# Two transformer-style blocks on one core: norm roots taken from the bank, sums of ones put into TensorE's waits, and six smaller moves

## The reference, cut to what matters

```python
y = xf * lax.rsqrt(jnp.mean(xf * xf, axis=-1, keepdims=True) + EPS)      # each norm
hx = modulate(rmsnorm(x, norm_g[l]), shift[:, None], scale[:, None])
# odd layer
u, g = jnp.split(h @ p["w_in"], [W_POOL], axis=-1)
d = multiscale_pool(u.reshape(bn * rows, GRID_W, W_POOL)).reshape(bn, n, W_POOL)
y = jnp.einsum("bngi,gij->bngj", d, p["w_grp"]) * p["scale"]
x = x + gate * ((y * jax.nn.silu(g)) @ p["w_out"])
# second block
mix_x, _, _ = token_mixers(h @ w_in[l], ...)    # forward and backward chunked recurrence
x = x + mod[:, 2, None] * mix_x
h2 = modulate_2(rmsnorm_2(x, g_ffn[l]), mod[:, 3, None], mod[:, 4, None])
x = x + mod[:, 5, None] * swiglu(h2, w_up[l], w_down[l])
return rmsnorm_2(x, g_final)
```

## Time and profile before

| | us |
|---|---|
| median of the runs | 942.37 |
| profiled execution, its own time | 943.91 |
| its span, first to last instruction | 942.1 |
| TensorE busy (matrix products) | 891.3 (95%) |
| VectorE busy | 704.2 (75%) |
| ScalarE busy | 498.2 (53%) |
| GpSimd busy | 142.5 (15%) |
| mean granted TensorE clock | 0.974 of full |

### The profile page before, as it was taken

One profiled execution on the slowest core, in us unless ns is written; L12 is line 12 of the kernel. 1 busy time (PEld: TensorE's weight loads), 2 busy tenths in 40 slices (PEclk: granted clock), 3 DMA queues, 4 the chain that ended last, 5 costly groups with the idle time before them and its releaser, 6 DMA issues.

```text
span 942.1 us, 17236 instructions
## 1 busy us (share of the span) xinstructions
PE 891.3 (95%) x7064; PEld 833.2 (88%) x7064; DVE 704.2 (75%) x1017; ACT 498.2 (53%) x710; POOL 142.5 (15%) x254
## 2 busy tenths in 40 slices
PE   7999999998997699999999999979999799999995
PEld 5788777688997699989999999979999799999995
DVE  5687578999877599978579985776995876566553
ACT  5374888896544445325553574554534454444441
POOL 0004674710011001400212100300001000000000
PEclk8899999999998799999999999989999799999998
DMA  9935977986575668866628744625566466666661
GB/s 366 359 135 143 311 262 227 294 303 222 174 258 180 218 201 263 297 216 193 185 85 312 269 151 129 213 90 179 161 187 174 142 217 184 187 182 180 201 201 45
DMA packets 56013, 195.43 MB, mean 207 GB/s; under 512 B 7936, under 2 KB 9088, under 8 KB 54528
## 3 DMA queue, kind: packets, MB, share of 16 engines
q1 hardware_dynamic: 40320, 147.73, 49.2%
q0 software_dynamic: 15616, 46.61, 14.4%
HBM read 188.60 MB, written 1.05 MB: 201 GB/s over the span
## 4 chain that ended last, share of the span: by engine, by line
PE 67%; DVE 15%; ACT 7%; DMA 5%; issue 3%; POOL 2%; SPq 0%; DVEq 0%; ACTq 0%; POOLq 0%
PE ps L571 19%; PE ps L572 19%; PE ps L573 19%; DVE w_lo L1336 5%; PE ps L724 3%; ACT w_hi L944 2%; DMA m<-in_mod_w 2%; DMA raw<-in_stream 2%; POOL shifts L459 2%; PE px L644 1%; DMA modw<-in_mod_w 1%; PE ps L655 1%; DVE modw L1370 1%; DVE win L1350 1%; DVE dump L1706 1%
## 5 line engine op out<-in xcount | busy, mean ns | idle before, releaser
L1336 DVE TENSOR_TENSOR w_lo<-raw,w_hi 128x1024 fp32r<-128x1024 f32 x232 | 280.9, 1227 | 120.1 <-ACT w_hi L944 119.6
L944 ACT ACTIVATE w_hi<-raw 128x1024 fp32r<-128x1024 f32 x232 | 243.6, 1056 | 123.5 <-DMA raw<-in_stream 123.3
L571 PE MATMUL ps<-h_hi,w_hi 128*128 128x256 f32 (+1 forms) x928 | 278.5, 300 | 24.7 <-DVE w_lo L1336 13.5
L572 PE MATMUL ps<-h_lo,w_hi 128*128 128x256 f32 (+1 forms) x928 | 273.3, 295 | 0.0
L573 PE MATMUL ps<-h_hi,w_lo 128*128 128x256 f32 (+1 forms) x928 | 273.0, 294 | 0.0
L571 PEld LDWEIGHTS ps<-h_hi,w_hi 128*128 128x128 f32 x928 | 181.4, 195 | 37.2 <-DVE w_lo L1336 18.0
L572 PEld LDWEIGHTS ps<-h_lo,w_hi 128*128 128x128 f32 x928 | 181.5, 196 | 3.7 <-issue 1.2
L573 PEld LDWEIGHTS ps<-h_hi,w_lo 128*128 128x128 f32 x928 | 181.3, 195 | 2.8
L571 PE MATMUL ps<-h2o_hi,w_hi 128*128 128x256 f32 x352 | 102.1, 290 | 0.0
L573 PE MATMUL ps<-h2o_hi,w_lo 128*128 128x256 f32 x352 | 100.0, 284 | 0.0
L572 PE MATMUL ps<-h2o_lo,w_hi 128*128 128x256 f32 x352 | 99.9, 284 | 0.0
(11 more groups left out here) (332 smaller groups left out, 1736.7 us busy)
## 6 DMA issues: line engine op xcount, KB each, us to landing
raw<-in_stream SPq DMA_DIRECT2D x252, 512.0 KB, 3.9
modw<-in_mod_w POOLq DMA_DIRECT2D x80, 512.0 KB, 5.8
m<-in_mod_w SPq DMA_DIRECT2D x8, 1024.0 KB, 19.2
shifts<-upad POOLq DMA_DIRECT2D x128, 35.5 KB, 4.0
c_row<-in_c_rows SPq DMA_DIRECT2D x3, 512.0 KB, 6.1
ctxT<-in_ctxT SPq DMA_DIRECT2D x1, 1024.0 KB, 5.1
x<-in_xT SPq DMA_DIRECT2D x1, 1024.0 KB, 7.1
ctx2T<-in_ctx2T SPq DMA_DIRECT2D x1, 1024.0 KB, 6.6
```

What stands on the lines that cost most here:

```text
L571: pe.matmul(o, wh, hi, start=start, stop=False)
L572: pe.matmul(o, wh, lo, start=False, stop=False)
L944: act.activation(w_hi[split[0] % HI_RING][:], raw[n % RING][:], ACT.Copy).then_inc(w_hi_ready, 1)
L1336: v.tensor_tensor(w_lo[n % RING][:], raw[n % RING][:], w_hi[split[0] % HI_RING][:].bitcast(F32), ALU.subtract).then_inc(w_lo_ready, 1)
```

## The change

1. The norm's root for three norms (after `yb`, after `wo`, after `d2`) and for the context's norm is taken by ScalarE straight from the bank, with the scale and the small constant in the same instruction (`root_of_mean`); VectorE's scaling pass and one hand-over go. The root's table is loaded ahead of the squares (`root_table`).
2. `keep_busy(n)` puts n products of ones with ones (128 x 128) on TensorE: 18 of them in the start, and 4 before and 14 behind the sums of the norms after `yb` and `wo`.
3. ScalarE takes the first four `ou` tiles and the first two `ua` tiles out of their banks before the splits of later weights; two splits are run ahead of that.
4. `add_to_x` for the last tile of a layer (except `ob`) no longer runs the split of four tiles later first.
5. `keys_out(1, 0)` stands ahead of the copies of `o 2`, `o 3` and `ga2 0`.
6. VectorE splits `ou 6` and `ou 7` right behind the first `pooled`; in the feed-forward part it splits two more tiles before `mod_tiles(18, 0)`, and the four dot products of `mod_tiles(19, 0)` stand in the loop, one each at t = 2 to 5.
7. At the end ScalarE multiplies `x` by the last gain while TensorE still works (`xg`), VectorE multiplies by the reciprocal in three pieces, and three DMAs store them instead of eight.

```diff
@@ SyncE
-            for k in range(KT):
-                sp.wait_ge(stored, k + 1)
-                sp.dma_start(out[:, k, :], x[:, k, :]).then_inc(out_done, 16)
+            for n, (first, end) in enumerate(((0, 2), (2, 5), (5, 8))):
+                sp.wait_ge(stored, n + 1)
+                sp.dma_start(out[:, first:end, :], xg[:, first:end, :]).then_inc(out_done, 16)
@@ TensorE
+            def keep_busy(n, bank=px[1]):
+                for _ in range(n):
+                    pe.matmul(bank[:, 0:P], ones, ones, start=True, stop=True)
...
-            first_rows(0)
-            first_columns(0)
-            first_rows(1)
-            first_columns(1)
+            for k in range(2):
+                first_rows(k)
+                keep_busy(2, ps[3])
+                first_columns(k)
             for k in range(KT):
+                if k < 3:
+                    keep_busy((4, 8, 2)[k], ps[3])
                 if k + 2 < KT:
                     first_rows(k + 2)
...
+            keep_busy(4)
             two_chunks(px[0], sq1, 1, KT)
+            keep_busy(14)
...
+            keep_busy(4)
             two_chunks(px[0], sq4, 7, 5 * KT)
+            keep_busy(14)
@@ ScalarE
+            def root_table():
+                S.do(act.activation(warm, warm, ACT.Sqrt))
+            def root_of_mean(stat, t, bank):
+                act.wait_ge(stat_done, stat)
+                act.activation(t, bank[:, 0:T], ACT.Sqrt, scale=1.0 / D, bias=eps_col).then_inc(sd_ready, 1)
...
+            root_table()
             for t in range(KT):
                 done("yb", t)
                 squares("yb", t, sq1)
-            highs("ou", 3)
-            sqrt_of(4, vr1[:])
+            root_of_mean(5, vr1[:], px[0])
             shifted(0, h1_hi, t1, shift1)
             act.wait_ge(pads_ready, 1)
+            highs("ou", 5)
             for t in range(2 * KT):
-                done("ou", t)
+                if t < 4:
+                    act.wait_ge(tile_done, TILE[("ou", t)] + 1)
+                else:
+                    done("ou", t)
...
-            sqrt_of(8, lnv[:, 3, :])
+            sqrt_of(4, lnv[:, 3, :])
+            keys_out(1, 0)
+            highs("ga2", 2)
             out_of("o", 2, og2, ACT.Silu)
             out_of("o", 3, og2, ACT.Silu)
             out_of("ga2", 0, ga2, ACT.Sigmoid)
-            keys_out(1, 0)
...
             for t in range(KT):
                 done("d2", t)
                 squares("d0", t, sq5)
-            sqrt_of(11, v4[:, 0, :])
+                act.activation(xg[:, t, :], x[:, t, :], ACT.Identity, scale=col("g_final_2", t)).then_inc(xg_ready, 1)
+            root_of_mean(10, v4[:, 0, :], px[0])
@@ VectorE
             def add_to_x(name, t, gate):
-                done(name, t)
+                if t < KT - 1 or name == "ob":
+                    ahead(name, t)
+                v.wait_ge(tile_done, TILE[(name, t)] + 1)
...
-            def rstd(stat, bank, width, eps, t, dst, var_n):
-                v.wait_ge(stat_done, stat)
-                v.tensor_scalar(t, bank, 1.0 / width, eps, ALU.mult, ALU.add).then_inc(var_ready, 1)
-                v.wait_ge(sd_ready, var_n)
+            def rstd(n, t, dst):
+                v.wait_ge(sd_ready, n)
                 S.do(v.reciprocal(dst, t))
...
+            lows("ub", 2)
             mod_tiles(18, 0)
-            ahead("ua", 0)
-            mod_tiles(19, 0)
...
+                if 2 <= t < 6:
+                    mod_tiles(19, 0, t - 2, 1)
...
-            for k in range(KT):
-                v.scalar_tensor_tensor(out=x[:, k, :], in0=x[:, k, :], scalar=col("g_final_2", k), in1=v4[:, 1, :],
-                                       op0=ALU.mult, op1=ALU.mult).then_inc(stored, 1)
+            v.wait_ge(xg_ready, KT)
+            for first, end in ((0, 2), (2, 5), (5, 8)):
+                by_token = v4[:, 1, :].rearrange("p (n t) -> p n t", n=1).to_broadcast([P, end - first, T])
+                v.tensor_tensor(xg[:, first:end, :], xg[:, first:end, :], by_token, ALU.mult).then_inc(stored, 1)
```

More of the change, by code:

```diff
@@ L295, in build @@
         sq5 = at("sq5", W, [KT, T])
+        xg = at("xg", W + 8, [KT, T])
         ps = [ctx.enter_context(nc.psum_tensor(f"ps{j}", [P, 2 * T], F32)) for j in range(BANKS)]
@@ L362, in build @@
         out_done = sem("out_done")
+        xg_ready = sem("xg_ready")
         modA = columns(2 * KT).rearrange("p (k w) -> p k w", w=2)
@@ L595, in side_by_side @@
                             mm.then_inc(tile_done, 1)
+            def keep_busy(n, bank=px[1]):
+                for _ in range(n):
+                    pe.matmul(bank[:, 0:P], ones, ones, start=True, stop=True)
             pe.wait_ge(cc_clear, 2)
-            for n in range(12):
-                pe.matmul(px[n % 2][:, 0:P], ones, ones, start=True, stop=True)
+            keep_busy(12, ps[3])
             stats(px[2], lambda k: sq0[:, k, :], 0, sq0_ready)
@@ L858, in _ @@
             thirds("ga2", 0, *own2)
-            pe.wait_ge(var_ready, 6)
+            pe.wait_ge(var_ready, 4)
             pe.wait_ge(hg_dve, 10)
@@ L888, in _ @@
             pe.wait_ge(in_sgu, 48)
-            pe.wait_ge(var_ready, 7)
+            pe.wait_ge(var_ready, 5)
             for g in range(HEADS):
@@ L1123, in sqrt_of @@
                 S.n += 1
-                act.wait_ge(var_ready, n - 2)
+                act.wait_ge(var_ready, n)
                 S.sync()
                 act.activation(t, t, ACT.Sqrt).then_inc(sd_ready, 1)
-            sqrt_of(3, lnt[:, 3, :])
+            sqrt_of(1, lnt[:, 3, :])
             highs("gb", 5)
@@ L1186, in _ @@
                 act.activation(og[:, t, :], psum_of("og", t)[:, 0:T], ACT.Silu).then_inc(free_of("og", t), 1)
-            sqrt_of(5, vr[:, 0, :])
+            root_table()
+            root_of_mean(6, vr[:, 0, :], px[1])
             for t in range(KT):
@@ L1198, in _ @@
             highs("f", 3)
-            sqrt_of(6, vr[:, 1, :])
-            act.wait_ge(var_ready, 5)
+            sqrt_of(2, vr[:, 1, :])
+            act.wait_ge(var_ready, 3)
             act.activation(vr[:, 2, :], vr[:, 2, :], ACT.Sqrt).then_inc(sd_ready, 1)
@@ L1303, in _ @@
             highs("gb2", 3)
-            sqrt_of(9, ors[:])
+            sqrt_of(5, ors[:])
             for t in range(KT):
@@ L1311, in _ @@
                 squares("wo", t, sq4)
-            sqrt_of(10, v4[:, 0, :])
+            root_of_mean(9, v4[:, 0, :], px[0])
             shifted(3 * KT, h3_hi, t4, sh3)
+            highs("ub", 2)
             for t in range(FT):
-                done("ua", t)
+                if t < 2:
+                    act.wait_ge(tile_done, TILE[("ua", t)] + 1)
+                else:
+                    done("ua", t)
                 if t >= 4:
@@ L1676, in _ @@
             v.memset(opad[:, :, :, 8 + GRID_W:PW], 0.0).then_inc(pads_ready, 1)
-            rstd(5, px[0][:, 0:T], D, EPS6, vr1[:], vr1[:], 4)
+            rstd(4, vr1[:], vr1[:])
             modulate(0, x, vr1[:], sc1, shift1, t1, h1_hi, h1_lo)
@@ L1741, in _ @@
             pooled(0)
+            lows("ou", 7)
             second_pair(3)
@@ L1756, in _ @@
                     second_pair(pairs_after[t])
-            rstd(6, px[1][:, 0:T], D, EPS, vr[:, 0, :], vr[:, 3, :], 5)
+            rstd(5, vr[:, 0, :], vr[:, 3, :])
             for t in range(KT + 1):
@@ L1803, in _ @@
             v.tensor_scalar(vr[:, 0, :], vr[:, 1, :], EPS, None, ALU.mult).then_inc(var_ready, 1)
-            v.wait_ge(var_ready, 4)
+            v.wait_ge(var_ready, 2)
             v.wait_ge(stat_done, 8)
```

12 lines of the change are left out of this document (6 added, 6 removed).

## The result

The changed kernel takes 929.70 us, the median of four runs (927.22 to 930.44), against 942.89 for the kernel before on the same chip (four runs, 941.29 to 944.29). The ratio is 0.9856 [0.9831, 0.9881], so it is faster by 13.2 us. The forecast was 921.9 with a range of 916 to 929: the sign was right, the gain of 20.5 was put 7.3 us too high, and the time lies 0.7 outside the range. That the gain is 5.8 to 7.3 short of the forecast in all three is not.

The account below looks back on a forecast made before the run. TensorE (busy 891.3 of 942.1 us), its waits and half-clock time bound the kernel, with VectorE in `og`. Terms 2.4 + 2.9 + 8.6 - 0.8 + 5.0 + 0.9 + 1.5 = 20.5 off 942.4 gave 921.9, 80% range 916 to 929.

Parts of the forecast that it names:

- the first feed-forward tiles: Tiles after the norm after `wo`: `ff` wait of 1.3 us goes, split of `ua 3` late by 0 to 1.0; gain 0.9.
- A second premise: At the norm after `yb`: a 1.5 us wait leaves the clock at 1.0, as waits up to 2.4 did; 1.9 gained.
- The start: Kernel start: eighteen sums in the waits keep TensorE at full clock; gain 2.4 us, ends 0 and 2.9.
- The norms: Norms after `yb` and `wo`: earlier reciprocals and no fall of the clock; gains 2.9 and 5.0 us.
- the clock terms: Behind the norms after `yb` and `wo`: stretches at clock 0.5 go, gaining 1.9 and 2.6 us.
- The banks of `ou`: `ou` tiles: early bank copies cut the `w_lo` wait from 7.5 to 1.3 us; gain 8.6, lower end 4.
- a bound of 12.0: Norm after `yb` and `ou` tiles: the most they can give, from VectorE's waits of 8.9 and 3.1 us.
- The keys: Backward keys: `kdT` wait goes, a 6.3 us wait for `St` comes, clock falls; -0.8, ends -1.5 and +1.5.
- The rival of a full gain: Backward keys: if `St` did not hold them, gain 7.9 instead of -0.8, time 913.2; chance 8%.
- The end: Kernel end: root from the bank, fewer multiplications and three stores; gain 1.5 us, range 0.5 to 2.2.
- The table loads: Root's table loaded ahead of the squares, where ScalarE waits: 0 us, at worst 0.3.
- The rival that the sums don't hold the clock: Start and both norms: gains of 2.4, 1.9 and 2.6 fail and sums delay layers; 931.0, chance 12%.

## Why the prediction was right and wrong

**The step that failed** is the one on the first feed-forward tiles: "What is late next is the split of `ua 3`, whose weights load beside four 512 KB rows: 0 to 1.0 us." The mechanism was named and the size was wrong. I took +0.9 for these tiles. The pair of traces has -2.1: the wait of 1.26 for `ff` is gone, and one of 3.17 for the split of `ua 3` stands in its place (2.79 and 2.93 in the repeats). I had priced the collision from a trace in which the last row was issued 3.8 us before the load for `ua 3` was due. Two parts of the change itself closed that distance. The clock, now at 1.0 behind the norm, brings the load 2.6 us closer to the start of the layer (10.72 us behind it instead of 13.35). The two splits that VectorE now makes ahead of `mod_tiles(18, 0)` push the rows 2.7 us further from it (the first is 8.83 behind it instead of 6.14). So rows and loads were in flight together, and the load for `ua 3` took 7.6 us. That this lateness was the rows' doing is shown by spreading them: the load took 3.4 us and the time fell by 4.7. How the blame divides between the two parts was not tried one by one. In the kernel without the norms' sums the clock fell here and the load came 12.9 us behind the start of the layer, yet it took 6.8 us and TensorE waited 2.40, so the order of the splits makes most of it, as far as one trace tells.

**A second premise**, worked out at the norm after `yb` and kept for every short wait, was also wrong: "waits of up to 2.4 us elsewhere in the trace left the clock at 1.0". One execution showed that, and it was one draw. Of the thirteen profiled executions of the changed kernel and its variants, eight had a fall at the wait of 2.1 to 2.4 us near 233 (the kernel before had none there in its one), and four of eight with the wait at `ua 3` had one behind it. Another place is the wait of 1.30 us left when the state is copied first, with one fall in five profiles. I counted no loss for any of them. A pair of executions of the same kernel puts the falls at 1.1 and 2.6 us, and together they are most of the distance between the best run (925.96) and the worst (930.63). The profile of before lay 1.0 above the median of 942.89, and that of after 2.5 below its own; its mean granted clock was 0.993, and those of the other three executions 0.988 to 0.990. Together they make up the 3.5 us between the gain of the traces (16.7) and that of the medians (13.2).

**The start** (2.4): the sums do hold the clock (it stays at 1.0 from 7.16) and the kernel is 2.0 to 2.4 ahead by 147 to 160 us. But the next wait, at 194 us, ends with rows that have to land, and it grows from 1.04 to between 1.15 and 2.07; 1.0 is left at 234 in the first trace, and nothing in the medians, shown twice. VectorE's timeline has the two waits for these rows, which were 0.35 and 0.92 before:

```profile
187.29 1.23 DVE L1404 SCALAR_TENSOR_TENSOR modw<-modw,c_row 128x1024 f32<-128x1024 f32 x1 [1.13 <-DMA modw<-in_mod_w]
...
189.71 1.22 DVE L1404 SCALAR_TENSOR_TENSOR modw<-modw,c_row 128x1024 f32<-128x1024 f32 x1 [1.19 <-DMA modw<-in_mod_w]
```

Over all fourteen traces the picture is less sharp. The ten with the sums are 1.6 us ahead of the four without them at 190 us on average, 0.7 behind the wait at 192 to 195, and 0.6 behind the one at 233; the first of these waits is 0.51 to 2.20 us with the sums and 1.04 or less without. So most of the gain goes there, and the small rest can't be seen in medians. The bound below of 0 was there; I asked whether the clock would hold, not whether the time would be kept. That these rows alone set the wait was not tried.

**The norms.** Both latencies came out as worked (layer start 292.35 where 293.4 less the start's share was forecast, wait 1.33 for 1.5; and 0.94 for 1.1 after `wo`). The clock holds: 1.0 behind both in every profile with the sums. The Trainium skill (TensorE: Matmul & The Clock Gate, Part 1) has activity release the throttle, and the sums of ones count as such here. Against the kernel before, the clock terms came out too, by the loads' issue times: 1.8 for 1.9, and 2.6 for 2.6. But only a part of that is owed to the sums of ones. The old waits were longer and left 20 and 28 products at half speed; without the sums, the shortened waits of 4.3 and 4.1 us leave 24 and 15, and 0.9 of the first goes to VectorE. So the sums are worth 1.4 and 1.7 at most in the traces, and 2.3 in all by the medians, which isn't firm. In the change itself their worth can't be told from nothing.

**The banks of `ou`** (8.6, with the norm 11.5 under a bound of 12.0): 10.9 measured for the norm and these tiles together, 8.0 for the tiles alone in the pair and 7.9 when they are undone. Here the lists of VectorE's and ScalarE's work were followed to the microsecond, and the wait was 0.93 for 1.3.

**The keys** (-0.8): the new wait of 6.4 (6.3 forecast), the clock at 0.5 behind it, and a small loss: -0.6 in the pair of traces, -1.3 by undoing it. The rival of a full gain fell for the reason given, VectorE's order, and the kernel that changes this order gets 4.7 of the 8.7 that separated the two by its median, and 6.2 where the clock does not fall behind the 1.30 us that are left.

**The end** (1.5): 1.6. The Trainium skill (DMA: Bandwidth & Descriptors, Anatomy of one DMA) gives its 2.0 us for DMAs issued by GpSimd, and these stores are issued by SyncE: the gain of 1.1 estimated from it was 0.5 too small, and nothing in the sum rests on it. The table loads: no cost seen.

The rival that the sums don't hold the clock (931.0) comes nearest in time, but its cause is refuted by the granted clock; the right number would have been reached by wrong means.

## What to carry to other kernels

A gain is kept only as far as the next wait whose end is set by something else, so for each microsecond won, look at the next two or three waits and ask what ends them: a load's issue, another engine's list, or TensorE itself. When a stage gets faster, or work is put ahead of other work, the distance between two requests for data changes: list what is then issued within the same few microseconds as the load on the critical path (here the distance went from 3.8 us to nothing, and the load from 4 to 7.6 us). And read the clock behind a wait of 1 to 3 us as a chance, not as a fact of one trace: either price it at half, or profile the same kernel two or three times before leaning on it.

## What the hardware showed that was not expected

- The same wait lets the granted clock fall or not, from one execution to the next of one kernel: behind 2.43 us at 233, 19 products in 3.41 us at 0.5 in one, and 31 at 1.0 in the other. Behind a wait of 1.30 us at 617 it fell in one of five. At the start the clock fell in all four profiles without the sums, behind waits of 0.8 to 2.2 us, and in none of the ten with them.
- A 512 KB load took 3.4 to 7.2 us to land when the rows were spread, and 4.2 to 11.7 when eleven such requests went out between 730.7 and 745.8; 356 GB/s were moved in the six microseconds from 742.6.
- Sums of ones with nothing waiting for them, 3.29 us of them in waits that are 4.33 and 4.06 us long without them, held the clock in every profile and delayed the next layer by nothing (6.07 us from the last sum into `x` with and without).
